# State stores issued by SyncE, sample value products merged and moved ahead, and reciprocal roots of short norms by a power on GpSimd

## The chip, the cores and the metric

The kernel runs on one core of a Trainium2 chip. The metric is the device time of one execution in microseconds (us). The engines named below are TensorE (PE, with its weight loads as PEld), VectorE (DVE), ScalarE (ACT), GpSimd (POOL) and SyncE (SP), which only issues transfers here. Sixteen DMA engines move the data; SP's transfers and ACT's transfers stand on a queue each.

## The reference

Two layers work on a prompt of 512 tokens and on 8 sample tokens that bring states and caches. Each layer has a mixer with three parts (an HGRN scan, an mLSTM and dilated window attention), an output projection, and a feed-forward part (dense in layer 0, 8 experts in layer 1). What the change touches:

```python
def head_rmsnorm(x, g):
    B, T, H, Dh = x.shape
    y = x * lax.rsqrt(jnp.mean(x * x, axis=-1, keepdims=True) + EPS)
    return y.reshape(B, T, H * Dh) * g.astype(F32)
...
    S_h, o_h = hgrn_chunk(st['hgrn'], *args_h)
    (C_m, n_m, m_m), o_m = mlstm_chunk((st['C'], st['n'], st['m']), q_m, k_m, v_m, ig, lf)
    out_m = head_rmsnorm(o_m, lp['ml_g']) * jax.nn.sigmoid(mo.astype(F32))
...
    p = jnp.exp(s - mx)                                   # sample tokens, three window groups
    o = jnp.einsum('nthj,ntjhd->nthd', p, vg) / den[..., None]
    new_buf = jnp.concatenate([buf, jnp.stack([k, v], axis=2)], axis=1)[:, T:]
...
    x = x + mix @ lp['w_out']
    x = x + ffn_fn(rmsnorm(x, lp['n2']), *ffn_p)
...
    y_prompt = rmsnorm(xp, final_norm_g)
```

The states `S_h`, `C_m`, `n_m` and `m_m` and the shifted caches `new_buf` are outputs too.

## The kernel before

The order of the work is written out by hand, one program for each engine; semaphores tie them together. Weights come in units of 128 output columns: SP loads a unit into one of three raw buffers (`load`, L516), ACT rounds it (`hi`, L777), POOL or DVE makes the rest (`lo`, L637; `split_lo`, L409), and PE multiplies (`passes`, L1189). `load` of unit u waits until PE has finished unit u-3. The output projection has 8 units; its units 0 to 2 are loaded long ahead, and units 3 to 7 are loaded one by one as earlier units end.

In the mixer PE's work comes in jobs (`mixer_jobs`), which take the 8 banks of PSUM in turn: job n waits until the reader of job n-8 has released its bank (`Job`). Towards the end of the mixer, per layer: `decays` makes the score products (jobs md, mqk) and DVE scales them (`decayed`, L2187); `outputs` makes numerators (mi, mo) and DVE divides them (`finish`); `mean_squares` (L1860, L1861) sums the squares of a pair of heads, ACT takes the reciprocal root as an Ln and an Exp (`head_rms`, L859, L860; L993, L994 for the sample tokens), DVE multiplies (`normalise`, L1866; L2242 for the sample tokens), PE transposes (`turn_heads`, jobs mt 2 to 4) and DVE applies the gate (`gate_heads`, L1874). The job wv multiplies the 8 samples' window probabilities (`spw`) with their cached values (`cv`): 24 products, for each sample one over 128 keys and one each over 64 and 16 keys of the two other groups. When the last gate is done, ACT issues the six state stores (L1006) and rounds the mixer's output for the output projection (L1009), and POOL makes the rest of it (L694).

SP's program at the end of layer 0's mixer, after the loads of the sample states, in its own order:

```python
                    if li == 0 and n == RAW - 1:
                        sp.wait_ge(state_in, 64)
                        for l2 in range(2):
                            for g, w in enumerate(WB):
                                sp.dma_start(a[f"cache{g}_s"][l2, :, 0:w - 1, :, :], a[f"cache{g}"][l2, :, 1:w, :, :]
                                             ).then_inc(shift_dma, 16)
                        for e in range(8):
                            sp.dma_start(rows_in[e * SLOTS:(e + 1) * SLOTS, :], a["zero"]).then_inc(cleared, 16)
```

These are six copies that shift the caches of both layers in DRAM (L588), each with a leading dimension of 8 samples, and eight fills that clear the experts' row buffer (L591). Behind them SP issues the loads of the output projection's units 3 to 7.

In layer 1, before the experts, ACT takes the reciprocal root of the token norms (`rms`, L1071, L1072) between DVE's sum (L2311) and the router's logits (L2318). At the very end the same is done for the final norm: ACT squares five token tiles (L1172), then Ln and Exp over all five (L1173, L1174), then DVE scales the tiles (L2506) and SP stores them.

## Time and profile before

| | |
|---|---|
| median of 3 runs | 1847.91 us (1847.22 to 1848.05) |
| the profiled execution | 1849.23 us |
| its span (first to last instruction) | 1847.0 us |
| busy: PE, DVE, ACT, POOL | 1687.7 (91%), 954.0 (52%), 696.2 (38%), 391.3 (21%) us |
| chain that ended last | PE 81%, DVE 7%, POOL 4%, ACT 2%, DMA 1% of the span |
| PE's granted clock | 0.936 of full speed |
| moved by DMA | 271.42 MB, of it 250.52 MB on SP's queue and 10.62 MB on ACT's |

The span is what the profiler saw of one execution; the time of that execution is 2.2 us more. The busy shares are averages over stages with different limits; the chain that ended last tells which engine held up the end, stage by stage.

### The profile page before, as it was taken

How to read it: one execution, taken by the hardware profiler on the slowest of the kernel's cores; microseconds unless marked ns; L12 is line 12 of the kernel's file. 1: busy time of each engine (PE TensorE's matmuls, PEld its weight loads, DVE VectorE, ACT ScalarE, POOL GpSimd, SP SyncE). 2: the span in 40 equal slices, each digit the busy share in tenths (PEclk: the TensorE clock that was granted, in tenths of full speed). 3: DMA queues.
4: the chain of work that ended last, by engine and by line, in shares of the span. 5: the costliest groups of instructions: out<-in, count | busy, mean ns of one | idle time of the engine just before them, and what ended most of it. 6: DMA issues, size and time to landing. Idle time of an engine off the chain costs nothing.

```text
span 1847.0 us, 33779 instructions
## 1 busy us (share of the span) xinstructions
PE 1687.7 (91%) x13514; PEld 1625.7 (88%) x13514; DVE 954.0 (52%) x1433; ACT 696.2 (38%) x1050; POOL 391.3 (21%) x236
## 2 busy tenths in 40 slices
PE   6999978799999999998999877859999999999993
PEld 5999857789999999998998567859999999999993
DVE  5577676532210122226776765255746548457474
ACT  4533363342221223235333633443534435335342
POOL 4300250343443344443002503030000000000031
PEclk8999986699999999999999877969999999999997
DMA  4222227422222223222222212368778678677682
GB/s 176 81 70 77 74 72 266 188 80 92 92 87 86 81 92 105 79 81 69 69 77 78 70 50 86 112 211 277 241 246 288 217 255 290 216 266 259 234 313 75
DMA packets 71225, 271.42 MB, mean 147 GB/s; under 512 B 11668, under 2 KB 12404, under 8 KB 70300
## 3 DMA queue, kind: packets, MB, share of 16 engines
q1 hardware_dynamic: 63988, 250.52, 39.7%
q10 hardware_dynamic: 3464, 10.62, 1.8%
q0 software_dynamic: 3648, 8.53, 1.3%
q8 instruction: 89, 1.46, 0.3%
q14 instruction: 36, 0.29, 0.1%
HBM read 253.24 MB, written 36.34 MB: 157 GB/s over the span
## 4 chain that ended last, share of the span: by engine, by line
PE 81%; DVE 7%; POOL 4%; issue 3%; ACT 2%; DMA 1%; ACTq 0%; DVEq 0%; POOLq 0%; SPq 0%
PE psum L1189 39%; PE psum L1709 11%; PE psum L1719 10%; PE psum L1711 9%; PE psum L1236 9%; POOL r_cvt L674 2%; POOL r_w L676 1%; PE psum L1688 1%; PE psum L1241 1%; PE psum L1677 1%; DVE n L1780 1%; POOL r_cvt L675 1%; DVE r_bt L1964 0%; DVE acc L1767 0%; DMA wraw<-in_w_in 0%
## 5 line engine op out<-in xcount | busy, mean ns | idle before, releaser
L1709 PE MATMUL psum<-xg,xhi 128*128 128x320 f32 x1408 | 371.4, 307 | 1.2 <-issue 0.9
L1711 PE MATMUL psum<-xg,xlo 128*128 128x256 f32 x1408 | 369.7, 282 | 0.0
L637 POOL TENSOR_TENSOR wlo<-wraw,whi 128x1024 fp32r<-128x1024 f32 (+1 forms) x90 | 231.3, 2572 | 405.0 <-ACT whi L777 405.0
L1709 PEld LDWEIGHTS psum<-xg,xhi 128*128 128x128 f32 x1408 | 265.2, 188 | 3.5 <-issue 3.1
L1711 PEld LDWEIGHTS psum<-xg,xlo 128*128 128x128 f32 x1408 | 265.3, 188 | 0.0
L1189 PE MATMUL psum<-xnh,whi 128*128 128x260 f32 x1120 | 234.6, 291 | 32.1 <-POOL xnl L694 12.5
L777 ACT CAST whi<-wraw 128x1024 fp32r<-128x1024 f32 (+1 forms) x130 | 140.7, 1085 | 288.4 <-DMA wraw<-in_w_in 161.9
L415 DVE TENSOR_TENSOR xlo<-xraw,xhi 128x1024 fp32r<-128x1024 f32 x176 | 215.2, 1224 | 54.3 <-ACT xhi L1137 54.2
L1137 ACT CAST xhi<-xraw 128x1024 fp32r<-128x1024 f32 x176 | 182.7, 1048 | 142.1 <-PE psum L1711 142.0
L1189 PE MATMUL psum<-xnl,whi 128*128 128x260 f32 x1120 | 228.3, 286 | 0.0
L1189 PE MATMUL psum<-xnh,wlo 128*128 128x260 f32 x1120 | 228.2, 286 | 0.0
L1189 PEld LDWEIGHTS psum<-xnh,whi 128*128 128x128 f32 x1120 | 175.8, 192 | 38.3 <-issue 18.1
L1719 PE MATMUL psum<-eh,xraw 128*128 128x160 f32 x1408 | 199.7, 299 | 0.0
L1719 PEld LDWEIGHTS psum<-eh,xraw 128*128 128x128 f32 x1408 | 192.7, 190 | 0.0
L1189 PEld LDWEIGHTS psum<-xnl,whi 128*128 128x128 f32 x1120 | 175.9, 192 | 0.0
L1189 PEld LDWEIGHTS psum<-xnh,wlo 128*128 128x128 f32 x1120 | 175.5, 192 | 0.0
L1189 PE MATMUL psum<-xbh,whi 128*128 128x260 f32 x704 | 144.5, 286 | 1.9 <-issue 1.9
L1189 PE MATMUL psum<-xbh,wlo 128*128 128x260 f32 x704 | 141.9, 283 | 0.0
L1189 PE MATMUL psum<-xbl,whi 128*128 128x260 f32 x704 | 141.8, 283 | 0.0
L725 POOL DMA_INDIRECT yg<-rows_out,idx x10 | 15.5, 1551 | 542.9 <-DMA rows_out<-ytok 520.3
L1189 PEld LDWEIGHTS psum<-xbh,whi 128*128 128x128 f32 x704 | 108.5, 189 | 3.4 <-issue 2.1
L1189 PEld LDWEIGHTS psum<-xbh,wlo 128*128 128x128 f32 x704 | 108.6, 189 | 0.0
(427 smaller groups left out, 2422.1 us busy)
## 6 DMA issues: line engine op xcount, KB each, us to landing
xraw<-in_moe_gu SPq DMA_DIRECT2D x176, 512.0 KB, 4.2
xraw<-in_moe_dn SPq DMA_DIRECT2D x64, 704.0 KB, 5.8
wraw<-in_w_in SPq DMA_DIRECT2D x54, 512.0 KB, 3.2
wraw<-in_ffn_gu SPq DMA_DIRECT2D x44, 512.0 KB, 3.2
wraw<-in_ffn_dn SPq DMA_DIRECT2D x16, 704.0 KB, 4.1
wraw<-in_w_out SPq DMA_DIRECT2D x16, 512.0 KB, 3.5
out_cache_s<-in_cache SPq DMA_DIRECT2D x4, 2040.0 KB
rows_in<-in_zero SPq DMA_DIRECT2D x8, 640.0 KB, 33.8
```

The source lines that it names most:

```text
L415: eng.tensor_tensor(xlo[n % RWX][:, 0:KD * P], xraw[n % RWX][:, 0:KD * P], xhi[n % HIX][:, 0:KD * P].bitcast(F32), ALU.subtract).then_inc( ...
L637: pool.tensor_tensor(wlo[u % RAW][:, 0:cols], wraw[u % RAW][:, 0:cols], whi[u % SPL][:, 0:cols].bitcast(F32), ALU.subtract).then_inc(lo_ma ...
L674: step(pool.tensor_scalar(R["cvt"][:, 0:SEQ - n], mu[:, 0:SEQ - n], tap(j), None, ALU.mult))
L675: step(pool.tensor_scalar(R["cvt"][:, SEQ:T], cbuf[:, li, f, j, :], tap(j), None, ALU.mult))
L676: step(pool.tensor_tensor(out[:, n:SEQ], R["cvt"][:, 0:SEQ - n], out[:, n:SEQ], ALU.add))
L777: act.copy(whi[u % SPL][:, 0:cols], wraw[slot][:, 0:cols]).then_inc(hi_made, 1)
L1137: act.copy(xhi[n % HIX][:, 0:KD * P], xraw[n % RWX][:, 0:KD * P]).then_inc(hi_made, 1)
L1189: ins = pe.matmul(out[:, s, :], w[:, k * cols:(k + 1) * cols], x[:, k, s * H2:(s + 1) * H2], start=(k == 0 and first), stop=(k == kt - 1 a ...
L1236: self.last = pe.matmul(self.out(c0, n, rows, r0), lhsT, rhs, start=start, stop=stop, skip_group_check=True)
L1709: pe.matmul(epart(n), xhi[n % HIX][:, k * P:(k + 1) * P], xg[:, k, :], start=(k == 0), stop=False, skip_group_check=True)
L1711: ins = pe.matmul(epart(n)[:, 0:256], xlo[n % RWX][:, k * P:(k + 1) * P], xg[:, k, 0:256], start=False, stop=(k == KD - 1), skip_group_che ...
L1719: ins = pe.matmul(epart(n)[:, 0:SLOTS], xraw[n % RWX][:, k * P:(k + 1) * P], eh[:, k, :], start=(k == 0), stop=(k == KF - 1))
```

## The change

Four things are changed, in both layers where a layer is named.

1. The six state stores of a layer are issued by SP instead of ACT. SP waits for the job mt 2 and stands with them ahead of the cache copies, the fills and the loads of units 3 to 7.
2. The products of the sample values take 16 products instead of 24: `spw` gets 16 more columns so that the two small groups (64 and 16 keys) are one product over 80 rows with zeros between. The job wv moves from behind `outputs((4,))` to ahead of `outputs((2, 3))`, and DVE's use of it to behind `decayed(4)`.
3. The reciprocal roots of the head norms, of the norm ahead of the router and of the final norm move from ACT (Ln, Exp) to POOL (multiply and add, then a power of -0.5 against the tile `nhalf`). For the final norm this is done tile by tile, and DVE waits tile by tile.
4. ACT rounds the first units of the output projection as soon as the sample norm's sums are made and the last `outputs` job is done.

```diff
-    jobs += [("md", 2), ("md", 3), ("mqk", 2), ("mqk", 3), ("mi", 0), ("mi", 1), ("mo", 0), ("mo", 1), ("md", 4), ("mqk", 4)]
+    jobs += [("md", 2), ("md", 3), ("mqk", 2), ("mqk", 3), ("mi", 0), ("mi", 1), ("mo", 0), ("mo", 1), ("md", 4), ("mqk", 4), ("wv",)]
     jobs += [("mi", 2), ("mi", 3), ("mo", 2), ("mo", 3), ("co", 0), ("co", 1), ("mt", 2), ("mi", 4), ("mo", 4)]
-    jobs += [("wv",), ("mt", 3), ("fx",), ("mt", 4)]
+    jobs += [("mt", 3), ("fx",), ("mt", 4)]
...
-        spw, _ = at("spw", [P, 80])
+        spw, _ = at("spw", [P, 96])
+        nhalf, _ = at("nhalf", [P, 16])
...
                 sp.dma_start(R["cv"][:], a["cv"][li]).then_inc(state_in, 16)
+                made(sp, li, "mt", 2)
+                for name, src in (("hgrn_p", R["sall"][:, NC - 1, :, :]), ("mlstm_p", R["call"][:, NC, :, :]),
+                                  ("hgrn_s", flat(TQ, 3 * NB * 64)), ("mlstm_s", flat(TSV, 3 * NB * 65)),
+                                  ("m_p", proj[0:5, 5, SEQ - 1:SEQ]), ("m_s", R["sc8"][0:5, 32:40])):
+                    sp.dma_start(a[name][li], src).then_inc(S("state_out"), 16)
                 for n in range(RAW - 1, KD):
                     if n >= RAW:
                         load(U_OUT[li] + n, a["w_out"][li, n], KD * P)
@@ -660,6 +666,9 @@
...
+                if li == 0:
+                    bump(pool.memset(spw[:, 64:96], 0.0), S("spw_clear"), pool)
+                    step(pool.memset(nhalf[:], -0.5))
...
                 bump(pool.tensor_tensor(R["fr"][32:37, :], proj[0:5, 7, 0:SEQ], R["fr"][0:5, :].bitcast(F32), ALU.subtract),
                      S("fr_low"), pool)
+                for k, ss in enumerate((R["ss2"][:, 0:NC], R["ss2"][:], R["s10"][:], R["ss2"][:])):
+                    pool.wait_ge(S("ob_ms"), 4 * li + k + 1)
+                    step(pool.tensor_scalar(ss, ss, 1.0 / 64, EPS, ALU.mult, ALU.add))
+                    bump(pool.tensor_tensor(ss, ss, nhalf[0:ss.shape[0], 0:ss.shape[1]], ALU.pow), S("ob_rms"), pool)
                 if li == 0:
                     for n in range(SPL):
...
             for n in range(2, KD, 2):
                 split_lo(pool, U_OUT[1] + n, KD * P, lo_pool)
+            pool.wait_ge(S("squares_added"), 1)
+            step(pool.tensor_scalar(rms[:], rms[:], 1.0 / D, EPS, ALU.mult, ALU.add))
+            bump(pool.tensor_tensor(rms[:], rms[:], nhalf[:, 0:5], ALU.pow), S("rms_ready"), pool)
             pool.wait_ge(cleared, 128)
...
+            for t in range(5):
+                r = rms[0:tok(t), t:t + 1]
+                pool.wait_ge(S("last_squares"), t + 1)
+                step(pool.tensor_scalar(r, r, 1.0 / D, EPS, ALU.mult, ALU.add))
+                bump(pool.tensor_tensor(r, r, nhalf[0:tok(t), 0:1], ALU.pow), S("last_rms"), pool)
...
-            def head_rms(li, m):
-                act.wait_ge(S("ob_ms"), 3 * li + m - 1)
-                step(act.activation(R["ss2"][:], R["ss2"][:], ACT.Ln, scale=1.0 / 64, bias=K(C_EPS, 1)))
-                sig(act.activation(R["ss2"][:], R["ss2"][:], ACT.Exp, scale=-0.5), "ob_rms")
...
-                    ins = act.copy(spw[0:80, 64:80], bank("wp")[0:80, 64:80])
+                    if li == 0:
+                        act.wait_ge(S("spw_clear"), 1)
+                    step(act.copy(spw[0:64, 64:80], bank("wp")[0:64, 64:80]))
+                    ins = act.copy(spw[64:80, 80:96], bank("wp")[64:80, 64:80])
...
-                    if h in (3, 4):
-                        head_rms(li, h - 1)
-                act.wait_ge(S("obs_ms"), li + 1)
-                step(act.activation(R["s10"][:], R["s10"][:], ACT.Ln, scale=1.0 / 64, bias=K(C_EPS, 1, NB)))
-                sig(act.activation(R["s10"][:], R["s10"][:], ACT.Exp, scale=-0.5), "obs_rms")
-                head_rms(li, 4)
+                act.wait_ge(S("ob_ms"), 4 * li + 3)
                 made(act, li, "mo", 4)
                 for n in range(SPL):
                     hi(U_OUT[li] + n, KD * P)
...
                 taken(act, li, "mt", 4)
                 taken(act, li, "fx")
-                for name, src in (("hgrn_p", R["sall"][:, NC - 1, :, :]), ("mlstm_p", R["call"][:, NC, :, :]),
-                                  ("hgrn_s", flat(TQ, 3 * NB * 64)), ("mlstm_s", flat(TSV, 3 * NB * 65)),
-                                  ("m_p", proj[0:5, 5, SEQ - 1:SEQ]), ("m_s", R["sc8"][0:5, 32:40])):
-                    act.dma_start(a[name][li], src).then_inc(S("state_out"), 16)
-
                 for m in range(KD):
                     act.copy(xnh[:, m, :], proj[:, MIXT[m], :]).then_inc(mixh_made, 1)
...
-                    act.wait_ge(S("squares_added"), 1)
-                    step(act.activation(rms[:], rms[:], ACT.Ln, scale=1.0 / D, bias=K(C_EPS, 1)))
-                    sig(act.activation(rms[:], rms[:], ACT.Exp, scale=-0.5), "rms_ready")
+                    act.wait_ge(S("rms_ready"), 1)
...
-                step(act.activation(yg[0:n, t, :], xtok[0:n, t, :], ACT.Square, accum_out=rms[0:n, t:t + 1]))
-            step(act.activation(rms[:], rms[:], ACT.Ln, scale=1.0 / D, bias=K(C_EPS, 1)))
-            sig(act.activation(rms[:], rms[:], ACT.Exp, scale=-0.5), "last_rms")
+                sig(act.activation(yg[0:n, t, :], xtok[0:n, t, :], ACT.Square, accum_out=rms[0:n, t:t + 1]), "last_squares")
...
+                def values():
+
+                    pe.wait_ge(state_in, 64 * (li + 1))
+                    j = Job(li, "wv")
+                    own = spw[0:80, 64:96].rearrange("p (g c) -> p g c", g=2)
+                    for b in range(NB):
+                        c = 2 * b
+                        j.mm(c, 2, R["cv"][:, b, 0, :], spw[:, c:c + 2])
+                        j.last = pe.matmul(j.out(16, 32).rearrange("p (g c) -> p g c", g=2)[:, :, c:c + 2],
+                                           R["cv"][0:80, b, 1, :], own[:, :, c:c + 2], start=True, stop=True,
+                                           skip_group_check=True)
+                    j.end()
+
...
                 decays((4,))
+                values()
                 outputs((2, 3))
                 pe.wait_ge(S("decode_made"), 3 * li + 3)
                 query("co", R["qc8"], flat(TSV, 3 * NB * 65).rearrange("p (f b v) -> p f b v", f=3, b=NB), 65)
                 turn_heads(li, 2)
                 outputs((4,))
-                pe.wait_ge(state_in, 64 * (li + 1))
-                j = Job(li, "wv")
-                for b in range(NB):
-                    c = 2 * b
-                    j.mm(c, 2, R["cv"][:, b, 0, :], spw[:, c:c + 2])
-                    for g, (r, rows) in ((1, (0, 64)), (2, (64, 16))):
-                        j.mm(16 * g + c, 2, R["cv"][r:r + rows, b, 1, :], spw[r:r + rows, 64 + c:66 + c])
-                j.end()
...
                 finish(3)
                 decayed(4)
-                normalise(li, 3)
-                gate_heads(li, 2)
-                c8_out()
-                finish(4)
-                mean_squares(li, 4)
                 made(v, li, "wv")
                 for h in range(2):
                     r = slice(64 * h, 64 * h + 64)
@@ -2237,9 +2243,15 @@
                         free(ins, li, "wv")
                     else:
                         step(ins)
+                normalise(li, 3)
+                gate_heads(li, 2)
+                c8_out()
+                finish(4)
+                mean_squares(li, 4)
+                v.wait_ge(S("ob_rms"), 4 * li + 3)
+                sig(tt(R["obs"][:], R["obs"][:], bc(R["s10"][:].unsqueeze(2), NB, 10, 64), ALU.mult),
+                    "obs_normed")
                 gate_heads(li, 3)
-                v.wait_ge(S("obs_rms"), li + 1)
-                sig(tt(R["obs"][:], R["obs"][:], bc(R["s10"][:].unsqueeze(2), NB, 10, 64), ALU.mult), "obs_normed")
                 normalise(li, 4)
                 made(v, li, "fx")
                 fx = bank("fx")[:, 0:64].rearrange("p (m b) -> p m b", b=NB)
@@ -2500,9 +2512,9 @@
...
-            v.wait_ge(S("last_rms"), 1)
             for t in range(5):
                 n = tok(t)
+                v.wait_ge(S("last_rms"), t + 1)
                 stt(yg[0:n, t, :], xtok[0:n, t, :], rms[0:n, t:t + 1], gft[0:n, :], ALU.mult, ALU.mult).then_inc(y_made, 1)
```

On SP the rows below are its transfers in layer 0 from the load of the cached values (`r_cv`) to the output projection's first load behind them (`wraw` from `in_w_out`), before:

```order
L576 DMA r_cv<-in_cv 128x2048
L588 DMA out_cache_s<-in_cache 8x2x16256 [waits state_in]
L588 DMA out_cache_s<-in_cache 8x4x16320 x2
L588 DMA out_cache_s<-in_cache 8x2x16256
L588 DMA out_cache_s<-in_cache 8x4x16320 x2
L591 DMA rows_in<-in_zero 16x10240 x8
L516 DMA wraw_52<-in_w_out 128x1024 [waits unit_done]
L516 DMA wraw_53<-in_w_out 128x1024 [waits unit_done]
```

and now:

```order
L582 DMA out_hgrn_p<-r_sall 128x192 [waits job_done]
L582 DMA out_mlstm_p<-r_call 128x195
L582 DMA out_hgrn_s<-proj 128x1536
L582 DMA out_mlstm_s<-proj 128x1560
L582 DMA out_m_p<-proj 5x1
L582 DMA out_m_s<-r_sc_184 5x8
L594 DMA out_cache_s<-in_cache 8x2x16256 [waits state_in]
L594 DMA out_cache_s<-in_cache 8x4x16320 x2
L594 DMA out_cache_s<-in_cache 8x2x16256
L594 DMA out_cache_s<-in_cache 8x4x16320 x2
L597 DMA rows_in<-in_zero 16x10240 x8
L517 DMA wraw_52<-in_w_out 128x1024 [waits unit_done]
```

The six stores, with a wait for a job of PE, stand ahead of the six copies and the eight fills, and all of these stand ahead of the load.

On PE, at the end of `decays((4,))` and around the job wv (`spw`, `r_cv`), before:

```order
L1236 MATMUL psum<-r_bt,r_kh 128x128 [waits bank_read6]
L1236 MATMUL psum<-r_bt,r_kh 128x128 x3
L1236 MATMUL psum<-r_call,r_bt 128x65 [waits bank_read0,bank_read7]
L1236 MATMUL psum<-r_call,r_bt 128x65 x7
...
L1236 MATMUL psum<-r_va,r_qd 128x65 [waits bank_read6,bank_read7]
L1236 MATMUL psum<-r_va,r_qd 128x65 x3
L1236 MATMUL psum<-spw,r_cv 128x2 [waits bank_read0,state_in]
L1236 MATMUL psum<-spw,r_cv 128x2 x23
L1241 MATMUL psum<-cst,r_ob 128x128 [waits ob_normed,bank_read1]
L1241 MATMUL psum<-cst,r_ob 128x128 x3
```

and now:

```order
L1241 MATMUL psum<-r_bt,r_kh 128x128 [waits bank_read6]
L1241 MATMUL psum<-r_bt,r_kh 128x128 x3
L1241 MATMUL psum<-spw,r_cv 128x2 [waits bank_read7,state_in]
L1552 MATMUL psum<-spw,r_cv 128x2x2
L1241 MATMUL psum<-spw,r_cv 128x2
L1552 MATMUL psum<-spw,r_cv 128x2x2
...
L1241 MATMUL psum<-r_call,r_bt 128x65 [waits bank_read1,bank_read0]
L1241 MATMUL psum<-r_call,r_bt 128x65 x7
L1241 MATMUL psum<-r_va,r_qd 128x65 [waits bank_read7,bank_read2]
```

The job wv follows the score products directly, on bank 7, which the scaled product of head 2 has to release; `outputs((2, 3))` (`r_call`, `r_bt`) comes behind it.

On DVE, from `decayed(4)` (`r_qd`) to the last normalisations (`r_ob`, `r_ss`) before:

```order
L2187 TENSOR_TENSOR r_qd<-psum,r_dw 128x512 [waits bank_read5,job_done,dve_step]
L1866 TENSOR_TENSOR r_ob<-r_ob,r_ss_182 128x512 [waits ob_rms,bank_read6]
L1874 SCALAR_TENSOR_TENSOR proj<-psum,prm,proj 64x512 [waits gates_made,job_done,ob_normed]
...
L1861 TENSOR_REDUCE r_ss_182<-r_sqo 128x8 [waits dve_step]
L2235 TENSOR_TENSOR proj<-psum,st_69 64x3x8 [waits job_done,ob_ms]
L2235 TENSOR_TENSOR proj<-psum,st_69 64x3x8 [waits dve_step]
L1874 SCALAR_TENSOR_TENSOR proj<-psum,prm,proj 128x512 [waits gates_made,job_done,bank_read0]
L2242 TENSOR_TENSOR r_obs<-r_obs,r_s_196 8x640 [waits obs_rms,bank_read1]
L1866 TENSOR_TENSOR r_ob<-r_ob,r_ss_182 128x512 [waits ob_rms,obs_normed]
```

and now:

```order
L2198 TENSOR_TENSOR r_qd<-psum,r_dw 128x512 [waits bank_read5,job_done,dve_step]
L2241 TENSOR_TENSOR proj<-psum,st_70 64x3x8 [waits job_done,bank_read6]
L2241 TENSOR_TENSOR proj<-psum,st_70 64x3x8 [waits dve_step]
L1877 TENSOR_TENSOR r_ob<-r_ob,r_ss_183 128x512 [waits ob_rms,bank_read7]
L1885 SCALAR_TENSOR_TENSOR proj<-psum,prm,proj 64x512 [waits gates_made,job_done,ob_normed]
...
L1872 TENSOR_REDUCE r_ss_183<-r_sqo 128x8 [waits dve_step]
L2252 TENSOR_TENSOR r_obs<-r_obs,r_s_197 8x640 [waits ob_rms,ob_ms]
L1885 SCALAR_TENSOR_TENSOR proj<-psum,prm,proj 128x512 [waits gates_made,job_done,obs_normed]
L1877 TENSOR_TENSOR r_ob<-r_ob,r_ss_183 128x512 [waits ob_rms,bank_read1]
```

DVE's use of wv (`st`) stands right behind `decayed(4)`, and the last normalisations follow the last sum of squares without it between.

## Rows read from the trace of the kernel before

**Rows 1.** Chain that ended last, layer 0's mixer end: start us, us, engine, line.

```profile
311.13 0.70 DVE r_qd L2187
...
312.69 10.87 PE psum L1236 x96
...
323.56 1.04 PE psum L1241 x4
...
342.17 2.73 DVE r_ob L1866
...
347.01 0.36 ACTq L1006
...
349.23 0.32 ACTq L1006
...
351.72 4.34 PE psum L1189 x20
```

**Rows 2.** SP's issues in order of time, layer 0: start us, us, line, names, count.

```profile
285.94 4.39 SPq L588 DMA_DIRECT2D out_cache_s<-in_cache  x6
290.38 5.76 SPq L591 DMA_DIRECT2D rows_in<-in_zero  x8
359.44 0.34 SPq L516 DMA_DIRECT2D wraw<-in_w_out  x1
```

**Rows 3.** DMA view: the 4th, 5th and 8th fill, us from issue to landing.

```profile
rows_in<-in_zero SPq DMA_DIRECT2D x1, 640.0 KB, 17.1
rows_in<-in_zero SPq DMA_DIRECT2D x1, 640.0 KB, 50.6
rows_in<-in_zero SPq DMA_DIRECT2D x1, 640.0 KB, 58.4
```

**Rows 4.** Timeline, output projection of layer 0, units 2 and 3.

```profile
362.63 1.05 ACT L777 CAST whi<-wraw 128x1024 fp32r<-128x1024 f32 x1 [8.71 <-DMA wraw<-in_w_out]
363.76 2.40 POOL L637 TENSOR_TENSOR wlo<-wraw,whi 128x1024 fp32r<-128x1024 f32 x1 [7.02 <-ACT whi L777]
371.05 0.70 DVE L2298 TENSOR_TENSOR xT<-psum,xT 128x520 f32<-128x520 f32 x1 [3.14 <-PE psum L1189]
```

**Rows 5.** Windows, the products on spw alone: PE, PEld busy (count), PEclk.

```profile
1111.00:1112.00 1.00, 1.00 (x8) 0.95 (x8) 0.00 (x0) 0.00 (x0) 1.00 0.00 0
1116.00:1117.00 1.00, 1.00 (x5) 0.97 (x5) 0.00 (x0) 0.00 (x0) 0.50 0.00 0
```

**Rows 6.** Timeline, layer 1's mixer end to the output projection.

```profile
1096.04 1.42 DVE L2187 TENSOR_TENSOR r_qd<-psum,r_dw 128x512 f32<-128x512 f32 x2
1110.07 10.23 PE L1236 MATMUL psum<-spw,r_cv 128*128 128x2 f32 x48
1115.55 0.69 DVE L1861 TENSOR_REDUCE r_ss<-r_sqo 128x8 f32<-128x512 f32 x1
1123.71 0.69 DVE L1866 TENSOR_TENSOR r_ob<-r_ob,r_ss 128x512 f32<-128x512 f32 x1
1126.52 0.36 ACTq L1006 DMA_DIRECT2D out_hgrn_p<-r_sall  x1
1132.58 0.77 PE L1189 MATMUL psum<-xnh,whi 128*128 128x260 f32 x2 [6.94 <-POOL xnl L694]
```

**Rows 7.** Timeline, ahead of the router.

```profile
1198.12 1.20 DVE L2315 COPY xtok<-psum 8x1024 f32<-8x1024 f32 x1
1200.24 0.19 DVE L2318 TENSOR_TENSOR rl<-psum,rms 128x32 f32<-128x32 f32 x1 [0.92 <-ACT rms L1072]
```

**Rows 8.** Timeline, the final norm.

```profile
1831.40 2.47 DVE L2424 SCALAR_TENSOR_TENSOR xtok<-yg,gate,xtok 128x1024 f32<-128x1024 f32 x2 [0.28 <-DMA yg<-rows_last,idx]
1834.92 0.19 ACT L1172 ACTIVATION_READ_ACCUMULATOR yg<-xtok 8x1 f32 x1
1838.28 6.06 DVE L2506 SCALAR_TENSOR_TENSOR yg<-xtok,rms,gft 128x1024 f32<-128x1024 f32 x5 [4.41 <-ACT rms L1174]
```

**Rows 9.** A group of POOL's small operations: busy us, mean ns, idle before.

```profile
L677 POOL TENSOR_TENSOR r_w<-r_cvt,r_w 128x8 f32<-128x8 f32 x18 | 4.8, 269 | 1.4
```

More of the change, by code:

```diff
@@ L1864, in normalise @@
                 ob, ss2 = heads_of(m)
-                v.wait_ge(S("ob_rms"), 3 * li + m - 1)
+                v.wait_ge(S("ob_rms"), 4 * li + (1, 2, 4)[m - 2])
                 sig(tt(ob, ob, bc(ss2.unsqueeze(2), P, NC if m == 2 else 2 * NC, 64), ALU.mult), "ob_normed")
@@ L2181, in c8_out @@
                     step(tt(R["sq8"][:], R["obs"][:], R["obs"][:], ALU.mult))
-                    sig(v.tensor_reduce(R["s10"][:], R["sq8"][:], AX, ALU.add), "obs_ms")
+                    sig(v.tensor_reduce(R["s10"][:], R["sq8"][:], AX, ALU.add), "ob_ms")
                 def decayed(h):
```

## Prediction

> **What bounds the kernel now.** I read the chain that ended last first: PE carries 81% of it, so an edit counts only where PE waits for somebody. Four such places are touched: the end of the mixer in each layer, the wait ahead of the router, and the final norm. For each I read the order of time around it.
>
> In layer 0 the chain runs through DVE's scaled products, PE's outputs and the transposition mt 2, ends in normalisations and a gate on DVE, and passes through six store issues on ACT before PE can start the output projection at 351.72 [rows 1]. Layer 1 has the same shape: PE's products for wv take 10.23 us and end at 1120.3, DVE has its last sum of squares at 1116.24, the stores begin at 1126.52 and PE starts at 1132.58 [rows 6]. Ahead of the router DVE waits 0.92 us for ACT's roots [rows 7], and at the end 4.41 us [rows 8].
>
> Then I looked at what the SP queue holds, because the change puts a wait into it. In layer 0 SP issues the six cache copies from 285.94 and the eight fills from 290.38, and its next transfer is the load of output unit 3 at 359.44, when PE has ended unit 0 [rows 2]. The landings of the fills are the important rows [rows 3]. They were issued within 5.8 us, yet the fourth took 17.1 us, the fifth 50.6 and the eighth 58.4. So four fills' worth of completions came by about 310 and the rest between about 344 and 354. A fill runs on all engines, while the copies have a leading dimension of 8. The reading is that eight of the sixteen DMA engines had no copy and finished their share of the fills at once, while the other eight served the fills only after the copies ahead of them. A transfer on SP's queue therefore stands behind what SP issued earlier on the same DMA engine. The last fill landed at 295.5 + 58.4 = 353.9, that is 68.0 us after the first copy was issued. That is 5.5 us ahead of the first load behind it: the copies are hidden today, with almost nothing to spare.
>
> **State stores on SP, layer 0.** This is the largest term, and it is a loss. SP now waits for the job mt 2 before the stores, and copies, fills and the loads of units 3 to 7 are queued behind that wait. When is mt 2 done? wv needs the bank that the scaled product of head 2 releases, at 311.13 + 0.70 = 311.83 [rows 1]; with 0.14 for the hop it starts at 312.0. Its 16 products are 32 passes (24 were 48, [rows 6]); at the half clock 5 to 6 pass in a microsecond, at the full clock 8 [rows 5]. I take the half clock, which holds at that place, and 6.0 us (bounds 4 to 6.4): 318.0. The outputs of heads 2 and 3 and the sample query take 10.87 and mt 2 takes 1.04 [rows 1]: 329.9. The six issues take 347.01 to 349.55 = 2.54 us on ACT [rows 1], so the first copy leaves at 332.4 instead of 285.9, 46.5 us late. With the same 68.0 us the last fill lands at 400.4; I take 400, with 390 to 404 as bounds (the low one if the stores, which used to run beside the last fills, cost part of the 68 us, and the copies meet less traffic; the high one if the stores ahead of the copies cost their own time in full).
>
> The load of unit 3 needs all sixteen engines. It is issued near 357 and lands after the fills. From its issue to ACT's rounding it took 3.2 us before (359.44 to 362.63, [rows 2, 4]); some of that overlaps the queue, so I take 1.5 us after the fills. Rounding 1.05 and POOL's rest 2.40 with their hops [rows 4] bring PE's unit 3 to 400 + 1.5 + 3.6 = 405.1. Before, PE went on to unit 3 at 371.0 [rows 4]: +34.1. PE stands still for more than 30 us meanwhile. The first unit after today's wait took 359.44 - 351.72 = 7.7 us against (371.05 - 359.45) / 2 = 5.8 for the next ones [rows 1, 2, 4]: +1.9. Loads 4 and 5 wait in the same queue and land right behind, so only one stall arises. Layer 0: **+36.0**. All that layer 0's mixer gains ahead of it is swallowed, since the stall's end is set by the copies; an earlier mt 2 helps one for one.
>
> The Trainium skill (DMA: Bandwidth & Descriptors, "Queues, rings and completion order" and "Why a DMA increments its semaphore by 16 and not by 1") says that SP owns one ring on each DMA engine, that an engine takes descriptors in ring order, and that a leading dimension of 8 uses the eight lowest engines. The two steps in the fills' landings agree with it.
>
> **The mixer's end in layer 1**, where no copies follow. wv can begin when the product of head 2 is scaled, 1096.75, about 0.7 us before the outputs could (they need both halves of the 1.42 us, [rows 6]). With 6.0 us of wv ahead of them the outputs, and DVE's chain after them, move back by 5.3 us, and DVE's use of wv (0.4 by estimate, the size of a small DVE operation with its hop) now stands ahead too: the last sum of squares ends at 1116.24 + 5.7 = 1121.9. Behind it come the sample product, a gate, the last normalisation, its transposition and the last gate, 4.3 us with hops (0.8 + 0.8 + 0.7 + 1.1 + 0.8, sizes estimated from [rows 6] and from what the same kinds take): 1126.2, against 1126.5 before. So merging and moving the products gives next to nothing here: they leave the end and push the middle. POOL's roots (two small operations; the nearest row has 0.27 for one [rows 9]; the power has no row and I take 1.0 us for a pair with hops, bounds 0.6 and 3) lie beside the sample product and a gate. The normalisation may meet POOL's first rest of weights, which now starts right when the last root is made: the same operation took 2.73 us in layer 0, where POOL worked beside it, and 0.69 in layer 1 [rows 1, 6]; that is 2.0 us, and the chain would end at 1128.2. The Trainium skill (SBUF — State Buffer, "Who interferes with whom") has this as a lock: a DVE instruction with two SBUF inputs and a GpSimd instruction that reads SBUF exclude each other; by it the late end would be the result.
>
> What remains is the stores' issue on ACT. From their first issue to PE's start it was 6.06 us in layer 1; in layer 0 rounding and rest took 351.72 - 349.55 = 2.17 [rows 1, 6], so 3.9 of the 6.06 are issues, and these vanish. Gain between 3.9 - 1.7 = 2.2 and 3.9 + 0.3 = 4.2. I take **-2.5**, near the case with the collision. The earlier stores also let SP's next loads of layer 1 leave earlier; they are hidden either way.
>
> **Ahead of the router.** ACT's table loads and roots go, but DVE has a copy until 1199.32 anyway, and its next step was at 1200.24 [rows 7]: **-0.9**, not the whole of ACT's part. POOL's pair has more than 2 us of cover from DVE's two copies; a pair of 3 us would lose the gain.
>
> **Final norm.** ACT's last square ends at 1835.11 and DVE's scaling started at 1838.28; DVE itself was free at 1833.87 [rows 8]. Tile by tile DVE can start near 1834, and the fifth root (1835.1 + 1.0) is ready long before its turn. At best 1838.28 - 1834.0 = 4.3 is gained; if POOL's ten small operations and DVE's five alternate strictly, 5 x (1.2 + 0.9) fills the old end and nothing is gained. I take **-3.3**.
>
> Small costs: three memsets and one more small copy on ACT, less than 1 us, on engines that wait there anyway: 0.
>
> **Sum.** +36.0 - 2.5 - 0.9 - 3.3 = +29.3. The profiled execution took 1849.23, 1.3 above the median of the runs, so it becomes 1878.5 and the median 1847.9 becomes **1877**.
>
> **Rivals.** (a) The loads are not held: transfers of one queue share the engines, or unit 3 lands before PE wants it. Then layer 0 gains about 2 as layer 1 does (POOL has three rests to make there before the mixer's), and the sum is -2.0 - 2.5 - 0.9 - 3.3 = -8.7: 1839. It decides if the load issued near 357 lands by about 364. The two steps of the fills' landings speak against it. The Trainium skill's rule for it (same DMA page, "Issuing engines are not separate DMA queues") is that the choice of the issuing engine saves only sequencer time; it does not speak of what is queued behind a wait. Chance 0.10. (b) Held, but the copies drain some 15 us faster than before: 1862. Nothing in the rows says so, but the transfers beside them differ. 0.06. (c) Held, and POOL's roots are slow, 3 us or more a pair: the gains of layer 1, router and final norm go, 36.0 + 0 to 4: 1884 to 1888. Nothing shows the power's price. 0.08. (d) The gains and the stall cancel (the drain ends near 373): no change, 0.01. The forecast, held with the 68 us as they are, 0.75.
>
> **Chances and range.** About 0.2% (4 us) is what a measurement of this kernel can tell from no change. Slower: 0.75 + 0.06 + 0.08 = 0.89. Same: 0.01. Faster: 0.10. The range takes the forecast's bounds (copies' end 390 to 404, gains 0 to 9) and leaves out (a) and the ends of (b) and (c): 1862 to 1887.
>
> **What would show it.** Right: the first cache copy is issued near 332 and the eighth fill lands near 400; PE idles about 36 us ahead of unit 3 of layer 0's output projection, and the release named there is a load of `w_out`, through ACT and POOL; layer 1's output projection starts 2 to 4 us earlier relative to its mixer; the wait of 4.4 us at the end shrinks to 1 or less. Wrong: the load of unit 3 lands within 10 us of its issue while fills are outstanding, or POOL's pairs take several microseconds.

## The result and the profile after

The changed kernel takes 1896.11 us (median of 4 runs, 1895.56 to 1898.59) against 1847.98 us for the kernel before beside it: a ratio of 1.0261, with a 95% interval of 1.0244 to 1.0279, or 48 us more. The forecast was 1877 with a range from 1862 to 1887. The sign was right, the size was not. The profiled execution took 1895.98 us, its span is 1894.2. One run of the last kernel below, wv_back_act_roots, took 1870.42 us at a lower granted clock (0.87 against 0.94) and is left out of its ratio.

The stall in layer 0 is the forecast's largest term. The chain that ended last shows it (start, us, engine and line):

```profile
311.51 0.70 DVE r_qd L2198
...
312.35 0.56 PE psum L1241 x2
...
329.49 0.60 PE psum L1246 x4
...
349.84 8.74 PE psum L1194 x48
358.60 44.79 DMA wraw<-in_w_out
...
403.45 1.05 ACT whi L798
...
404.58 2.36 POOL wlo L643
...
407.07 22.98 PE psum L1194 x176
```

The first line answers to the first of [rows 1]. The products of wv start at 312.35, the transposition mt 2 ends at 330.09, PE runs units 0 to 2 from 349.84, and then one load of 44.79 us stands alone in the chain. SP's issues in order of time say why:

```profile
330.11 0.35 SPq L582 DMA_DIRECT2D out_hgrn_p<-r_sall  x1
...
334.02 4.73 SPq L594 DMA_DIRECT2D out_cache_s<-in_cache  x6
338.79 5.35 SPq L597 DMA_DIRECT2D rows_in<-in_zero  x8
358.60 62.19 SPq L517 DMA_DIRECT2D wraw<-in_w_out  x5
```

The stores start when mt 2 has ended, and the copies leave at 334.02, 48 us later than in [rows 2]. The load issued at 358.60 lands at 403.39. That is 69.4 us after the first copy. From 380 to 400 us the DMA engines are busy for 0.48 of their time only: the load waits behind the copies although half of the engines' time is free.

Layer 1's mixer end, in order of time; the three fences are DVE's, PE's and POOL's rows:

```profile
1137.52 1.42 DVE L2198 TENSOR_TENSOR r_qd<-psum,r_dw 128x512 f32<-128x512 f32 x2
...
1163.21 0.69 DVE L1872 TENSOR_REDUCE r_ss<-r_sqo 128x8 f32<-128x512 f32 x1
...
1166.63 2.86 DVE L1877 TENSOR_TENSOR r_ob<-r_ob,r_ss 128x512 f32<-128x512 f32 x1 [1.10 <-POOL r_ss L699]
...
1170.83 0.75 DVE L1885 SCALAR_TENSOR_TENSOR proj<-psum,prm,proj 128x512 f32<-128x512 f32 x1 [0.87 <-PE psum L1246]
```

```profile
1138.35 0.56 PE L1241 MATMUL psum<-spw,r_cv 128*128 128x2 f32 x2 [1.03 <-DVE r_qd L2198]
...
1174.12 0.77 PE L1194 MATMUL psum<-xnh,whi 128*128 128x260 f32 x2 [3.40 <-POOL xnl L707]
```

```profile
1164.05 0.75 POOL L698 TENSOR_SCALAR r_ss<-r_ss 128x8 f32<-128x8 f32 x1 [1.22 <-DVE r_ss L1872]
1164.89 1.64 POOL L699 TENSOR_TENSOR r_ss<-r_ss,nhalf 128x8 f32<-128x8 f32 x1
1166.60 2.34 POOL L410 TENSOR_TENSOR wlo<-wraw,whi 128x1024 fp32r<-128x1024 f32 x1
```

From DVE's scaled products to the output projection it is 1174.12 - 1137.52 = 36.60 us, where [rows 6] give 1132.58 - 1096.04 = 36.54. Nothing is gained there.

The router, the experts and the end (DVE's rows, then the experts' two lines of products on PE):

```profile
1240.72 0.17 DVE L2330 TENSOR_TENSOR rl<-psum,rms 128x32 f32<-128x32 f32 x1
...
1879.20 2.47 DVE L2436 SCALAR_TENSOR_TENSOR xtok<-yg,gate,xtok 128x1024 f32<-128x1024 f32 x2 [0.54 <-DMA yg<-rows_last,idx]
1885.45 6.05 DVE L2518 SCALAR_TENSOR_TENSOR yg<-xtok,rms,gft 128x1024 f32<-128x1024 f32 x5 [3.78 <-POOL rms L773]
```

```profile
L1720 PE MATMUL psum<-xg,xhi 128*128 128x320 f32 x1408 | 378.4, 313 | 0.9 <-issue 0.5
L1722 PE MATMUL psum<-xg,xlo 128*128 128x256 f32 x1408 | 376.7, 282 | 0.0
```

The kernel before has these two lines of products as follows:

```profile
L1709 PE MATMUL psum<-xg,xhi 128*128 128x320 f32 x1408 | 371.4, 307 | 1.2 <-issue 0.9
L1711 PE MATMUL psum<-xg,xlo 128*128 128x256 f32 x1408 | 369.7, 282 | 0.0
```

The wait ahead of the final scaling, 4.41 us in [rows 8], is still 3.78, and the same products in the experts take 7.0 us more on each line. The products of the two lines run in turn and their busy times overlap, so the two sevens are not to be added: the table below has 6.7 us for the whole stage. This has no term in the forecast.

Put end to end, the places show where the 47.2 us of the spans came from (the times are starts on the span's clock):

| place (start of) | before | after | difference | added there | forecast |
|---|---|---|---|---|---|
| layer 0's output projection | 351.72 | 349.84 | -1.9 | -1.9 | |
| first product of the dense layer | 405.4 | 443.0 | +37.6 | +39.5 | +36.0 for both |
| its last such product | 732.8 | 772.9 | +40.1 | +2.5 | 0 |
| layer 1, scaled product of head 2 | 1096.04 | 1137.52 | +41.5 | +1.4 | 0 |
| layer 1's output projection | 1132.58 | 1174.12 | +41.5 | +0.1 | -2.5 |
| router's `rl` | 1200.24 | 1240.72 | +40.5 | -1.1 | -0.9 |
| last product of the experts | 1817.1 | 1864.3 | +47.2 | +6.7 | 0 |
| scaling of the final norm | 1838.28 | 1885.45 | +47.2 | 0.0 | -3.3 |

### The profile page after: what moved, and what is told of

The parts are those of the page before. It is cut to its first block, busy times and chain, and to the rows that moved or that the text cites. A ratio compares the mean times of both kernels' runs of the same rounds, so it can differ in the third digit from the quotient of the medians.

```text
span 1894.2 us, 33714 instructions
## 1 busy us (share of the span) xinstructions
PE 1694.1 (89%) x13482; PEld 1632.9 (86%) x13482; DVE 961.2 (51%) x1433; ACT 665.3 (35%) x1012; POOL 416.9 (22%) x266
## 4 chain that ended last, share of the span: by engine, by line
PE 79%; DVE 7%; POOL 6%; DMA 4%; issue 3%; ACT 2%; DVEq 0%; POOLq 0%; SPq 0%; ACTq 0%
PE psum L1194 38%; PE psum L1720 11%; PE psum L1730 10%; PE psum L1722 9%; PE psum L1241 8%; DMA wraw<-in_w_out 2%; POOL r_cvt L683 2%; POOL r_w L685 1%; PE psum L1699 1%; PE psum L1688 1%; PE psum L1246 1%; POOL wlo L643 1%; POOL r_cvt L684 0%; DVE n L1791 0%; DVE r_bt L1975 0%
## 5 line engine op out<-in xcount | busy, mean ns | idle before, releaser
L1720 PE MATMUL psum<-xg,xhi 128*128 128x320 f32 x1408 | 378.4, 313 | 0.9 <-issue 0.5
L1722 PE MATMUL psum<-xg,xlo 128*128 128x256 f32 x1408 | 376.7, 282 | 0.0
L1722 PEld LDWEIGHTS psum<-xg,xlo 128*128 128x128 f32 x1408 | 270.9, 192 | 0.0
L1194 PEld LDWEIGHTS psum<-xbl,whi 128*128 128x128 f32 x704 | 109.3, 190 | 2.6 <-issue 2.6
```

Of the source, the lines that this page charges most:

```text
L1194: ins = pe.matmul(out[:, s, :], w[:, k * cols:(k + 1) * cols], x[:, k, s * H2:(s + 1) * H2], start=(k == 0 and first), stop=(k == kt - 1 a ...
L1720: pe.matmul(epart(n), xhi[n % HIX][:, k * P:(k + 1) * P], xg[:, k, :], start=(k == 0), stop=False, skip_group_check=True)
L1722: ins = pe.matmul(epart(n)[:, 0:256], xlo[n % RWX][:, k * P:(k + 1) * P], xg[:, k, 0:256], start=False, stop=(k == KD - 1), skip_group_che ...
```

## Experiments

Twelve kernels, in five groups; each time stands beside runs of the kernel before on the same chip.

**1. Is the stall the queue, and nothing else?** In the changed kernel SP issues the copies and fills ahead of the wait again (copies_first):

```diff
+                if li == 0:
+                    sp.wait_ge(state_in, 64)
+                    ... (six copies, eight fills)
                 made(sp, li, "mt", 2)
                 ... (six stores)
```

> The changed kernel, but on SP the six cache copies and the eight fills are issued ahead of the wait for mt 2 and the stores, as they stood before. Theory (head of the queue): the copies leave near 286 and are drained near 354 again, the load of unit 3 lands about 3 to 4 us after its issue, PE goes from unit 2 to unit 3 without a stall, some 19.3 us after its start at 349.8 instead of 57.2 us: 38 us are won back and the time is about 1858. Rival (the stores themselves, or what else changed in the mixer, delay the loads): unit 3 still lands tens of us late and the time stays above 1885.

1857.29 us, ratio 1.0042 (1.0025 to 1.0059): 39 us are won back. SP's rows, then ACT's rounding of unit 3:

```profile
286.70 4.39 SPq L582 DMA_DIRECT2D out_cache_s<-in_cache  x6
...
331.51 0.35 SPq L590 DMA_DIRECT2D out_hgrn_p<-r_sall  x1
...
358.60 23.39 SPq L517 DMA_DIRECT2D wraw<-in_w_out  x5
```

```profile
361.82 1.05 ACT L798 CAST whi<-wraw 128x1024 fp32r<-128x1024 f32 x1 [9.55 <-DMA wraw<-in_w_out]
```

The load is issued at the same 358.60 and its data is rounded at 361.82 instead of 403.45. The theory holds: where the copies and fills stand in SP's order makes the stall.

The other way round, the kernel before gets only the late copies; its stores stay on ACT (before_late_copies):

```diff
                         sp.wait_ge(state_in, 64)
+                        made(sp, li, "mt", 2)
                         for l2 in range(2):
```

> The kernel before with one edit: SP waits for the job mt 2 ahead of the six cache copies; the stores stay on ACT, the products and the roots are as before. Theory (the copies' late start is the whole stall): mt 2 ends at 324.6, the copies leave then, the load of unit 3 lands 69.4 us later (as in the changed kernel, from 334.02 to 403.39), near 394, and PE starts unit 3 near 398 instead of 371: 27 us and some 1 to 2 us for the clock after it, 1875 to 1878. Rival (the stores on SP's queue, which stood ahead of the copies, took part of the time): the copies drain sooner and the time is under 1868.

1882.99 us, ratio 1.0184 (1.0167 to 1.0201); the profiled execution took 1879.6. SP's issue of the copies, ACT's rounding and PE's unit 3:

```profile
323.92 4.39 SPq L589 DMA_DIRECT2D out_cache_s<-in_cache  x6
```

```profile
397.38 1.04 ACT L778 CAST whi<-wraw 128x1024 fp32r<-128x1024 f32 x1 [44.45 <-DMA wraw<-in_w_out]
```

```profile
400.99 0.77 PE L1190 MATMUL psum<-xnh,whi 128*128 128x260 f32 x2 [30.27 <-POOL wlo L638]
```

One added wait on SP makes the stall, without a store on SP. The data came 397.3 - 323.9 = 73.4 us after the first copy, 4 more than expected (why is not shown), so that the time lies above the range given. The rival, that stores ahead of the copies lengthen the drain, is out: with the stores it took 69.4.

**2. Where do the experts lose 6.7 us?** `spw` and `nhalf` take 128 bytes more per partition, and every tile allocated behind them moves by that. Three kernels move tiles and change no instruction: `top[0] += 128` behind `spw` in the kernel before, the same with 64, and `top[0] += 128` behind `nhalf` in the changed one, which makes it 256 against before. A fourth moves only `xhi`, the experts' rounded weights, and the tiles allocated behind it (the router's small tiles and the experts' working tiles for the gate):

```diff
-        xhi = [... slots[RWX + n])[0] for n in range(HIX)]
-        o = scr_off + 6 * KF * P * 4
+        xhi = [... slots[RWX + n] + 128)[0] for n in range(HIX)]
+        o = scr_off + 6 * KF * P * 4 + 128
```

> The kernel before with one edit: 128 bytes per partition are left free behind spw, so that every tile allocated behind it stands where it stands in the changed kernel. No instruction differs. Theory (placement in SBUF): a pair of the experts' products (L1709 and L1711) takes 0.2665 instead of 0.260 us although the clock is full, the experts take 6.6 us more, the dense layers and layer 1's mixer up to 4 more: 1854 to 1858. Rival (the slower experts come from transfers or from an order of time that the stores changed): no difference, 1848.

> The changed kernel with 128 more bytes per partition left free behind nhalf, so that the tiles behind it are moved by 256 bytes against before. No instruction differs. Theory (placement, with a period of 256 bytes or less that divides it): the pair of products takes 0.260 us again and 6.6 to 10 us are won: 1886 to 1889.5. Rival 1 (any move of these tiles away from where they were costs the same): 1896. Rival 2 (not a matter of placement): 1896, and the kernel before with the shift alone is not slower.

> The kernel before with 64 instead of 128 bytes left free behind spw. Theory 1 (any place other than the one modulo 256 bytes costs): the pair of the experts' products takes 0.2665 us again, 1854 to 1855. Theory 2 (only a particular place, such as the half of 256 bytes, costs): 0.260 us and 1848.

> The kernel before with only the experts' three buffers of rounded weights (xhi) and the router's small tiles behind them moved by 128 bytes; the mixer's tiles, the activations and the raw weights stay. Theory (the place of the weights that PE loads is what counts): the pair takes 0.2665 us, 1854 to 1855. Rival (another of the moved tiles, such as the raw buffers or the accumulators): 0.260 us, 1848.

| kernel | us | ratio to before, interval | busy us on the two lines |
|---|---|---|---|
| before_shift128 | 1854.91 | 1.0032, 1.0019 to 1.0044 | 378.3, 376.7 |
| before_shift64 | 1854.98 | 1.0044, 1.0030 to 1.0059 | 377.0, 375.3 |
| before_xhi128 | 1855.21 | 1.0042, 1.0025 to 1.0059 | 377.7, 376.0 |
| after_shift256 | 1887.73 | 1.0209, 1.0192 to 1.0226 | 370.6, 368.7 |

The groups of products on PE, first of before_xhi128, then of after_shift256:

```profile
L1709 PE MATMUL psum<-xg,xhi 128*128 128x320 f32 x1408 | 377.7, 312 | 1.0 <-issue 0.9
L1711 PE MATMUL psum<-xg,xlo 128*128 128x256 f32 x1408 | 376.0, 282 | 0.0
```

```profile
L1721 PE MATMUL psum<-xg,xhi 128*128 128x320 f32 x1408 | 370.6, 306 | 1.1 <-issue 0.7
L1723 PE MATMUL psum<-xg,xlo 128*128 128x256 f32 x1408 | 368.7, 281 | 0.0
```

Placement it is. The kernel before gets slower by it without another instruction, the changed kernel gets 8.4 us faster by 128 more bytes, and moving `xhi` (with the tiles behind it, which no product of these two lines reads) is enough. A shift of 64 bytes costs about as much as one of 128, so the second theory of before_shift64 fell; 256 costs nothing. The dense layer is not touched by the shift: from the first to the last product of `xbh` and `whi` it is 327.6 us in before_shift128 and 327.4 before.

**3. What holds the final norm?** DVE's branch on the overflow flag stands between its last sum and the scaling. The kernel after_no_branch leaves it out on DVE:

```diff
-            with v.If(v.value_load(flag[0:1, 0:1], min_val=0, max_val=1) > 0):
-                with v.Fori(0, NPASS - 1) as k:
-                    ...
```

> The changed kernel, without DVE's branch on the overflow flag ahead of the final norm (the further passes of the experts, which these inputs don't take, are left out on DVE alone). Theory (the branch covers the tile by tile scaling): DVE's first scaling starts when its last sum ends or at the latest when tile 0's root is there, near 1882 instead of 1885.45, and the end comes about 3 us earlier: 1893. Rival (DVE waits for POOL's five roots, which end at 1884.8): the first scaling still starts after the last root, 1896.

1895.17 us, ratio 1.0252 (1.0235 to 1.0269) beside 1.0261: the time can't tell it from the changed kernel, the trace can. DVE's rows, then POOL's:

```profile
1879.40 2.47 DVE L2436 SCALAR_TENSOR_TENSOR xtok<-yg,gate,xtok 128x1024 f32<-128x1024 f32 x2 [0.59 <-DMA yg<-rows_last,idx]
1881.91 2.48 DVE L2513 SCALAR_TENSOR_TENSOR yg<-xtok,rms,gft 128x1024 f32<-128x1024 f32 x2
1884.82 1.28 DVE L2513 SCALAR_TENSOR_TENSOR yg<-xtok,rms,gft 128x1024 f32<-128x1024 f32 x1 [0.43 <-POOL rms L773]
1886.82 1.28 DVE L2513 SCALAR_TENSOR_TENSOR yg<-xtok,rms,gft 128x1024 f32<-128x1024 f32 x1 [0.71 <-POOL rms L773]
```

```profile
1884.88 1.28 POOL L772 TENSOR_SCALAR rms<-rms 128x1 f32<-128x1 f32 x1
1886.24 0.54 POOL L773 TENSOR_TENSOR rms<-rms,nhalf 128x1 f32<-128x1 f32 x1
```

The first scaling starts 0.04 us after the last sum instead of 3.78: the branch was the cover. But now DVE and POOL alternate. POOL's multiply, 0.19 us in the changed kernel where it runs alone (1882.17), lasts 1.28, as long as DVE's scaling beside it, and a tile takes 2.0 us instead of 1.2. Counted from the last sums' start, the scaling begins 1881.91 - 1879.40 = 2.5 us later instead of 6.2, but ends 1890.07 - 1879.40 = 10.7 later instead of 12.3: of 3.7 us at the start 1.6 are left at the end.

**4. What are the stores and the products worth by themselves?** The kernel before with only the stores moved to SP, behind copies and fills (before_stores_sp); the diff is that of copies_first with the stores taken from ACT.

> The kernel before with the six stores of each layer issued by SP behind the copies and the fills instead of by ACT; products and roots as before. Theory (ACT's six issues lie on the path): 3.9 us less in layer 1 and 2.5 in layer 0, where the rows of before have them at 2.5, and the same end of the mixer: 1841 to 1842.5. Rival (something else, a load or POOL's rest, is right behind the issues): within 2 us of 1848.

1842.93 us, ratio 0.9967 (0.9957 to 0.9978): -6.1 us. From the end of the last gate to the output projection it is 347.89 - 345.72 = 2.2 us instead of 4.7 in layer 0, and 1126.95 - 1124.40 = 2.5 instead of 6.1 in layer 1, together -6.1. The theory holds; the time lies 0.4 above the range given.

Then the changed kernel with both mendings, copies first and 256 bytes (mended), and the same with the merged products back in their old place, both in the job list, in PE's program and in DVE's (mended_wv_back):

```diff
-    jobs += [..., ("md", 4), ("mqk", 4), ("wv",)]
+    jobs += [..., ("md", 4), ("mqk", 4)]
...
-    jobs += [("mt", 3), ("fx",), ("mt", 4)]
+    jobs += [("wv",), ("mt", 3), ("fx",), ("mt", 4)]
...
-                values()
                 outputs((2, 3))
...
                 outputs((4,))
+                values()
```

> The changed kernel with both mendings: copies and fills ahead of the wait, and the tiles moved by 256 bytes. Theory (the two are independent): 1857.3 less the 6.6 to 8.4 us of the placement, 1849 to 1851, so that all that the change was to bring, some 7 us, is not there. Rival (the mixer's gain shows up once the stall is gone): 1842.

> As mended, and the merged sample value products moved back to where they stood, behind outputs of head 4, with DVE's use of them behind the last sum of squares. Theory (the move pushes the middle of the mixer back by as much as it clears from its end, the merging alone gains): the last sum of squares ends some 7 us earlier in each layer, the products end at about the same time as that sum, and each layer's mixer ends 4 to 6 us earlier than in mended: 1838 to 1842. Rival (DVE and POOL at the mixer's end set the time wherever the products stand): within 2 us of mended.

mended: 1851.09 us, ratio 1.0008 (0.9999 to 1.0018). Without the queue and the placement the change brings nothing. mended_wv_back: 1838.73 us, ratio 0.9947 (0.9929 to 0.9965), 12.4 us less than mended, of which the start of the output projection shows 5.8 in layer 0 (343.74 against 349.49) and 7.1 in layer 1 (counted from the scaled product of head 2: 29.6 against 36.6). The move, not the merging, was the loss. In their old place the merged products do bring something: before_stores_sp, with 24 products there, takes 33.0 us for the same stretch (1126.95 - 1093.93), and DVE waits 4.16 us for them behind its last sum of squares, a wait that mended_wv_back doesn't have. The products themselves, in windows (busy us and count of PE and PEld, DVE, ACT, POOL, then the granted clock, the DMA engines' busy share and GB/s), first in the changed kernel, then in mended_wv_back:

```profile
1139.00:1145.00 6.00, 6.00 (x30) 6.00 (x30) 0.39 (x1) 0.83 (x3) 0.00 (x0) 0.50 0.01 3
```

```profile
1106.60:1109.60 3.00, 3.00 (x30) 3.00 (x29) 2.79 (x7) 0.48 (x1) 0.31 (x2) 1.00 1.01 410
```

Ahead of the outputs, right behind PE's wait for DVE, the 30 passes run at a granted clock of 0.50, the lower of the two levels (1.2 GHz), and take 6 us; in the old place, behind 12 us of products (from 1094.15 to 1106.59), they run at 1.00 (2.4 GHz) and take 3. There PE also has time for them, since DVE still works on its sums.

**5. Roots and rests.** Two variants of mended_wv_back: POOL's rest in layer 1 waits for DVE's last normalisation (wv_back_pool_after: one line, `pool.wait_ge(S("ob_normed"), 6)` ahead of `split_lo`), and the head and sample roots on ACT again (wv_back_act_roots: POOL's loop over the four roots out, `head_rms` and ACT's Ln and Exp for `s10` back).

> As mended_wv_back, but in layer 1 POOL's first rest for the output projection (2.34 us) waits until DVE's last normalisation is done. Theory (the two hold each other up): the normalisation takes 0.69 instead of 2.86 us, layer 1's output projection starts 2 us earlier against the last sum of squares, 1836.5. Rival (the 2.86 come from the operands or the roots' writes, not from POOL's rest): 2.86 again, and 1838.7 or more.

> As mended_wv_back, but the roots of the head norms and the sample norm stand on ACT again (Ln and Exp); the router's and the final norm's stay on POOL. Theory (a pair of POOL's operations and ACT's pair with its table loads cost about the same, 2.2 to 2.6 against 3.2 us, and in layer 0 ACT's rounding and POOL's rests come later behind ACT's roots): 1838 to 1842. Rival (POOL's power is what eats the gain of the mixer's end): 1835 or less.

wv_back_pool_after: 1834.23 us, ratio 0.9930 (0.9913 to 0.9947), the lowest median of all; its interval overlaps that of mended_wv_back, and layer 1's end accounts for 1 us of it only. DVE's rows, then POOL's:

```profile
1116.80 0.69 DVE L1879 TENSOR_TENSOR r_ob<-r_ob,r_ss 128x512 f32<-128x512 f32 x1
...
1117.77 2.26 DVE L2261 TENSOR_TENSOR proj<-proj,r_fx 128x40 f32<-128x40 f32 x1
```

```profile
1117.63 2.34 POOL L411 TENSOR_TENSOR wlo<-wraw,whi 128x1024 fp32r<-128x1024 f32 x1 [0.93 <-POOL r_ss L700]
```

The normalisation takes 0.69 instead of 2.86, as expected. But POOL's rest, which now starts at 1117.63, falls on the next operation of two inputs, which takes 2.26 instead of 0.20. From the last sum of squares to the last gate's start it is 5.4 us against 6.4: half of the 2 us expected. wv_back_act_roots: 1839.74 us, ratio 0.9960 (0.9944 to 0.9976), not to be told from mended_wv_back. Layer 1's end is 1.1 us shorter with ACT's roots (6.1 against 7.1 us from the last sum to the gate's end), layer 0's projection starts 1.7 later. Against ACT's roots POOL's power is neither a loss nor a gain in the whole time.

## Why the prediction was right in sign and wrong in size

The sum of the forecast was +29.3, the spans differ by 47.2. The table above splits the 17.9 between them. The stall, the one large term, was right; what failed are the steps around it. The result lies 9 us above the end of the range: a term that the prediction put at nothing (the place of the tiles, +6.7) and two gains that did not come (layer 1's mixer end and the final norm, 2.6 and 3.3) make up more than that. The range itself was added up a little wide at the bottom: its bounds (copies' end 390 to 404, gains 0 to 9) give 1865 to 1888.

- **The stall in layer 0: right.** Forecast: mt 2 done at 329.9, first copy at 332.4, unit 3 on PE at 405.1. Measured: 330.09, 334.02 and 407.07. The issues of the stores took 3.9 us on SP, not the 2.5 taken from ACT. Both experiments of group 1 show the cause. The Trainium skill's rule that each DMA engine takes the descriptors of a queue in ring order (DMA: Bandwidth & Descriptors, "Queues, rings and completion order") agrees with the 44.79 us of one load.
- **Missing from the sum: the placement, +6.7.** The step that failed is "small costs: 0": it counts the memsets and a copy. The diff shows two allocations, and I read them as columns for a product and a constant. That they move `xhi` was in the diff too, but no row of before can price it. The sum had no term and the range no bound for it. Shown by group 2.
- **Layer 1's mixer end: -2.5 forecast, +0.1 measured.** The stores' part was right: from the last gate's end to the projection it is 2.5 us now against 6.1. What failed is the chain ahead of it, put at 1126.2 to 1128.2 against 1126.5. It ends 3.6 us later than before (34.1 us from the scaled product to the last gate's end, 30.5 before); that the five parts behind the last sum add up to 4.2 and not to 4.3 plays no part. Two sizes are off: the products take 7.0 us (312.35 to 319.31 in layer 0) instead of 6.0, and POOL's pair took 2.5 us against my 1.0 (1164.05 to 1166.53), so that DVE waited 1.10 for it. The collision came in full, 2.86, but it was in the value taken; the pair's price was put near its lower bound (0.6 to 3), by a small POOL operation's row, and lies near the upper. The mechanism was seen, that the move pushes the middle as it clears the end, but not its price: mended_wv_back shows that the move costs 7 us here.
- **Final norm: -3.3 forecast, 0.0 measured.** The step that failed is "DVE can start near 1834". A load of the flag and a branch stand ahead of the scaling. In the trace of before they lie inside the 4.41 us that the view gives to ACT's roots (the branch's line: min/median/max in ns, first and last start):

```profile
L2498 DVEq TENSOR_LOAD <-flag x1: 550/550/550, 1833.9 to 1833.9; - x1
...
L2498 DVEq COMPARE_BRANCH  x1: 63/63/63, 1834.8 to 1834.8; - x1
```

  A wait named for one releaser covered a second one, of 3.8 us by the rows of the changed kernel, so that only some 0.6 us of the 4.41 could be gained. The wait is that much shorter now, and the last sum starts that much later. The rows of the load and the branch end at 1834.9; that the rest up to the scaling belongs to the branch, though no row shows it, is what after_no_branch shows. Its rows show too that the alternation, kept in the text as the worst case, is real.
- **Rival (c), slow roots, came nearest to the measured time, but not for its reasons.** Its 1884 to 1888 rest on pairs of 3 us or more that eat all gains. The pair in layer 1 took 2.5, the router's gain came, and the final norm's was lost to the branch.
- **The router: right,** -1.1 against -0.9, with DVE's copies as the bound and POOL's power (1.17 us) under them.
- **The dense layer, +2.5, and layer 1 up to its scores, +1.4: not forecast.** For the first the waits of PE in that stage (engine and line, released by: us, times, longest) show what is new:

```profile
PE psum L1194 <- issue: 2.4, 1, 2.4
PE psum L1194 <- DVE xT L2393: 1.4, 1, 1.4
```

  In the kernel before there is one such wait:

```profile
PE psum L1189 <- issue: 1.9, 1, 1.9
```

  Now PE waits 1.4, does a few products and waits 2.4 more with no releaser, and the granted clock is 0.91 over the 20 us around it where it was 1.00. The kernels with the old products have one wait there (1.7 to 2.0 us), those with the merged ones the second as well (2.3 to 2.9), so that the length or place of PE's program ahead of the loop suggests itself. That is argued, not shown. It is no small matter: in mended the dense layer's products of `xbh` and `whi` reach from 403.1 to 735.3, 4.8 us more than before, the largest loss left in that kernel. The placement is not the cause, by before_shift128. The 1.4 us stay open too.

## What to carry to other kernels

A wait put into a queue is priced by what stands behind it, not by what it guards: move the wait behind the transfers that need no wait, and the same stores on the same queue gain 6 us instead of costing 39. Before a product is moved ahead, look at what clock PE has there and who waits in the middle, since a stage's end can gain nothing while its middle goes back by as much. A changed tile size moves every tile behind it: pad it so that the weights keep their place modulo 256 bytes (256 is the one shift measured here that cost nothing), or measure the shift alone.

## What the runs showed of the hardware

- The pace of products depends on where the loaded weights lie in SBUF: at a granted clock of 1.00 (1300 to 1700 us) the experts' lines took 371.4 and 369.7 us with `xhi` in place, 377.0 to 378.4 and 375.3 to 376.7 when moved by 64 or 128 bytes, 370.6 and 368.7 when moved by 256. Only these products were seen to change.
- The load of a flag and a branch past a body that isn't run put 3.8 us between two operations of DVE (1881.67 to 1885.45); without them the gap is 0.04.
- The time of a power on POOL grows with the columns: the lines of the roots (min/median/max in ns, first and last start) show 1.04 us for 4 columns and 1.64 for 8 on 128 partitions, and 1.94 for 10 on 8 partitions:

```profile
L699 POOL TENSOR_TENSOR r_ss<-r_ss,nhalf x6: 1037/1638/1651, 309.9 to 1164.9; 128x8 f32<-128x8 f32 x4, 128x4 f32<-128x4 f32 x2
L699 POOL TENSOR_TENSOR r_s<-r_s,nhalf x2: 1943/1943/1943, 334.9 to 1160.9; 8x10 f32<-8x10 f32 x2
```

- DVE's operations with two inputs and POOL's hold each other up whole: 0.20 us become 2.26, 0.69 become 2.86, and POOL's 0.19 become 1.28, as the Trainium skill's rule has it (SBUF — State Buffer, "Who interferes with whom"). In wv_back_pool_after taking one collision away moved it to the next operation.
